# Looking up the chosen expert numbers with 16 operations of 50 candidates instead of three operations on a table of 800

## The reference, cut to what matters

```python
s1 = jnp.einsum('nhd,hkd->nhk', q[..., :PEER_HALF], k1)
s2 = jnp.einsum('nhd,hkd->nhk', q[..., PEER_HALF:], k2)
sc1, i1 = lax.top_k(s1, PEER_TOPK)
sc2, i2 = lax.top_k(s2, PEER_TOPK)
cand = (sc1[..., :, None] + sc2[..., None, :]).reshape(blk, PEER_HEADS, PEER_TOPK * PEER_TOPK)
top_sc, top_c = lax.top_k(cand, PEER_TOPK)
e1 = jnp.take_along_axis(i1, top_c // PEER_TOPK, axis=-1)
e2 = jnp.take_along_axis(i2, top_c % PEER_TOPK, axis=-1)
experts = e1 * N_KEYS + e2
gate = jax.nn.softmax(top_sc, axis=-1)
u_sel = u_tab[experts]
act = jax.nn.gelu(jnp.einsum('nd,nhkd->nhk', xt, u_sel).astype(jnp.float32), approximate=False)
z = (gate * act).astype(xt.dtype)
return jnp.einsum('nhk,nhkd->nd', z, v_tab[experts])
```

## Time and profile before

| | |
|---|---|
| median of three runs | 1917.72 us (1914.35 to 1924.69) |
| span of the profiled execution | 1749.2 us |
| the rest of the median, outside the span | 168.5 us |
| busy in the span: PE, DVE, ACT, POOL | 1093.8, 1073.7, 340.8, 1060.4 us |
| moved by the DMA engines | 659.75 MB, mean 377 GB/s |

### The profile page before, as it was taken

The page is one execution under the profiler, slowest core; times in us unless marked ns, Lnnn a source line. Parts: engine busy times, 40 slices in busy tenths (PEclk is TensorE's granted clock), DMA queues, the critical chain, the costliest instruction groups (busy, mean ns, idle before and its releaser), DMA issues.

```text
span 1749.2 us, 18263 instructions
## 1 busy us (share of the span) xinstructions
PE 1093.8 (63%) x6249; PEld 668.8 (38%) x6249; DVE 1073.7 (61%) x2724; ACT 340.8 (19%) x883; POOL 1060.4 (61%) x1131
## 2 busy tenths in 40 slices
PE   7968758988797989888853337743333333333344
PEld 6867736866675687566620001100000000000001
DVE  5636698765598187654347484848485757575420
ACT  3413223654132146403110000010000000000000
POOL 2005266665444566755567776677777777777771
PEclk9989878988898999989986568856666555665558
DMA  6579999899999999999999999999999999999997
GB/s 191 174 230 405 409 407 367 327 372 409 375 321 387 410 408 409 409 365 409 410 409 365 385 393 365 382 398 410 409 410 409 410 409 410 410 409 410 409 409 283
DMA packets 192850, 659.75 MB, mean 377 GB/s; under 512 B 32336, under 2 KB 32344, under 8 KB 192632
## 3 DMA queue, kind: packets, MB, share of 16 engines
q0 software_dynamic: 156672, 570.49, 83.2%
q1 hardware_dynamic: 35512, 86.01, 13.9%
q10 hardware_dynamic: 576, 2.10, 0.3%
HBM read 652.96 MB, written 5.16 MB: 376 GB/s over the span
## 4 chain that ended last, share of the span: by engine, by line
DMA 29%; PE 24%; POOL 21%; DVE 12%; issue 9%; ACT 2%; SPq 2%; ACTq 0%; POOLq 0%; DVEq 0%
POOL ring L609 15%; DMA ring<-in_u_experts,expert_idx 12%; PE pp L650 9%; DMA ring<-in_v_experts,expert_idx_by_token 7%; PE y L925 6%; DVE ring L1100 5%; PE pp L660 3%; PE pp L730 2%; POOL C_sample L609 2%; SPq L496 2%; DMA act_T<-in_v_experts,expert_idx_by_token 1%; POOL w_ring L609 1%; DMA w_ring<-in_w_all 1%; DMA w_ring<-in_u_experts,expert_idx 1%; DMA act_T<-in_u_experts,expert_idx 1%
## 5 line engine op out<-in xcount | busy, mean ns | idle before, releaser
L1100 DVE SCALAR_TENSOR_TENSOR ring<-ring,x_normed 128x1024 f32<-128x1024 f32 x440 | 530.1, 1219 | 345.2 <-DMA ring<-in_u_experts,expert_idx 341.0
L609 POOL DMA_INDIRECT ring<-in_u_experts,expert_idx x472 | 452.7, 959 | 399.0 <-DVE expert_idx L1480 123.7
L925 PE MATMUL y<-ring,z_columns 128*32 128x512 f32 x1328 | 411.5, 794 | 232.4 <-DMA ring<-in_v_experts,expert_idx_by_token 169.8
L609 POOL DMA_INDIRECT ring<-in_v_experts,expert_idx_by_token x308 | 304.7, 989 | 160.1 <-issue 75.0
L650 PE MATMUL pp<-act_T,w_ring 128*128 128x128 f32 (+2 forms) x1728 | 299.1, 332 | 43.5 <-DMA w_ring<-in_w_all 13.5
L650 PEld LDWEIGHTS pp<-act_T,w_ring 128*128 128x128 f32 x1728 | 266.3, 200 | 84.2 <-issue 49.6
L925 PE MATMUL y<-C_sample,z_columns 128*32 128x512 f32 x352 | 233.0, 926 | 66.0 <-DMA ring<-in_v_experts,expert_idx_by_token 51.8
L925 PE MATMUL y<-w_ring,z_columns 128*32 128x512 f32 x180 | 137.5, 984 | 181.6 <-DMA ring<-in_v_experts,expert_idx_by_token 161.5
L925 PEld LDWEIGHTS y<-ring,z_columns 128*32 128x32 f32 x1328 | 78.0, 131 | 400.0 <-issue 396.6
L660 PE MATMUL pp<-w_ring,act_T 128*128 128x128 f32 (+1 forms) x832 | 107.1, 291 | 27.8 <-DVE scratch L1297 10.8
L925 PEld LDWEIGHTS y<-w_ring,z_columns 128*32 128x32 f32 x180 | 21.4, 152 | 268.1 <-issue 268.1
(11 more groups left out here) (305 smaller groups left out, 1525.1 us busy)
## 6 DMA issues: line engine op xcount, KB each, us to landing
w_ring<-in_w_all SPq DMA_DIRECT2D x144, 512.0 KB, 6.9
ring<-in_u_experts,expert_idx POOLq DMA_INDIRECT x472, 11.0
ring<-in_v_experts,expert_idx_by_token POOLq DMA_INDIRECT x308, 10.0
x_res<-in_x_prompt SPq DMA_DIRECT2D x4, 512.0 KB, 7.9
C_sample<-in_state_C SPq DMA_DIRECT2D x4, 512.0 KB, 14.0
out_C_s<-C_sample ACTq DMA_DIRECT2D x4, 512.0 KB, 11.5
out_y_p<-x_res SPq DMA_DIRECT2D x16, 128.0 KB, 5.3
C_sample<-in_v_experts,expert_idx_by_token POOLq DMA_INDIRECT x80, 12.0
```

The source lines that it names most:

```text
L609: pool.indirect_dma_start(out=slot[s], out_offset=None, in_=a["u_experts"] if kind == "u" else a["v_experts"], in_offset=bass.IndirectOffs ...
L925: ins = pe.matmul(Y[low:low + 32, half * 512:(half + 1) * 512], zcols[:, part % 2, lo:lo + 32], rhs, start=False, stop=True, skip_group_ch ...
L1100: dve.scalar_tensor_tensor(out=slot[s], in0=slot[s], scalar=1.0, in1=xn_now[:, :] if t else xs[:, :], op0=ALU.mult, op1=ALU.mult, accum_ou ...
```

## The change

For each head, the two operations on a 16 x 50 table (compare, multiply) and the sum over it give way to one operation for each of the 16 picks. It compares the 50 positions with this pick's position, which comes as a scalar of one value per partition, multiplies by the 50 expert numbers, and adds up its own output through `accum_out` into the pick's place in `eid`. The waits between the three operations go, and one wait behind the sixteen stays.

```diff
             def experts_of(t, part, heads):
 
-                shape = [128, TOPK, CAND]
                 for h in heads:
-                    step(dve.tensor_tensor(hit, bc(iota[:, :], 1, shape), bc(posf[:, h, :], 2, shape), ALU.is_equal))
-                    step.done()
-                    step(dve.tensor_tensor(hit, hit, bc(ceid[:, h, :], 1, shape), ALU.mult))
-                    step.done()
-                    step(dve.tensor_reduce(eid[:, h, :], hit, AX.X, ALU.add))
+                    for k in range(TOPK):
+                        step(dve.scalar_tensor_tensor(out=hit[:, k, :], in0=iota[:, :], scalar=posf[:, h, k:k + 1], in1=ceid[:, h, :],
+                                                      op0=ALU.is_equal, op1=ALU.mult, accum_out=eid[:, h, k:k + 1]))
                     step.done()
                     between()
```

## The result

The changed kernel takes 1940.09 us (median of 6 runs, 1930.21 to 1946.03). The kernel before takes 1914.42 us (6 runs, 1902.76 to 1924.69, the three of the table ahead among them). The ratio is 1.0122, with a 95% interval of 1.0091 to 1.0152: about 23 us slower, and more than the 0.5% that a measurement can tell. The forecast was 1918.0 us and "same".

What follows compares the result with a forecast made beforehand. The gathers' start plus their bytes at a 409 GB/s DMA ceiling, plus losses below it, bounded the kernel. Adding 0.2 to 0.7 us for look-ups and subtracting up to 2.2 for POOL, little believed, gave 1918 us, range 1907 to 1935.

Steps and rivals of the forecast that it cites:

- The price of the new look-up alone: DVE's look-up: one operation every 0.188 us, 3.11 us a head against 3.07, 1.4 us more DVE work over 34 heads.
- a read that costs 0.07 us: Rival in DVE's look-up: the accumulator's read takes its own time, operations 0.255 us apart, 1923 to 1937 us; chance 0.15.
- no overlap: Rival in DVE's look-up: each operation waits for the previous read's end, 0.37 us each, 1932 to 1969 us; chance 0.08.
- the scalar is hidden: Rival in DVE's look-up: the scalar's load comes free, operations 0.127 us apart, 1902 to 1914 us; chance 0.06.
- the forecast of no change: Whole kernel: time the same within about 0.5% (9.6 us), at 1918 us; chance 0.74.
- the first line of "How the numbers follow": Whole kernel: 168.5 us lie between the profiled span of 1749.2 us and the median of 1917.7 us.
- 409 GB/s is what this traffic gets: DMA engines: 409 GB/s is the gathers' ceiling, held for the last third of the kernel.
- what DVE loses there is taken up: Between 1000 and 1200 us: POOL is ahead, so free slots absorb DVE delays of a few microseconds.
- The late look-ups: Twelve look-ups after 1040 us: on the recorded chain, but taken as running beside a full DMA queue.
- The sum: DVE's look-ups: 1.4 us more work over 34 heads, of which 0.2 to 0.7 us reach the end.
- bounded at 5 to 18 look-ups of 34: Look-ups before 560 us: five on the chain and 13 behind 265 us; between 5 and 18 pass their change on.

Runs made afterwards that it cites:

- e14: The changed kernel again, unedited, on a chip where the kernel before takes 1749.04 us: 1745.86 us, ratio 0.9992.
- e3: The changed kernel with its sixteen operations a head without accumulator, and one reduction over the table behind them: 1935.24 us, ratio 1.0102 to the kernel before.
- e0: The kernel before, unedited, profiled again on a chip of the slower kind: 1923.09 us, span 1921.3 us.
- e9: The kernel before with gathers of a quarter of each row's bytes (layer not computed): 1893.44 us, ratio 0.9885.
- e8: The kernel before with the sixteen operations only in the last nine parts (18 heads), the old look-up ahead of them: 1928.32 us, ratio 1.0060.
- e1: The kernel before with 29 added one-element multiplications behind each head's three look-up operations: 1951.83 us, ratio 1.0173.
- e4: The changed kernel with only the last of a head's sixteen operations incrementing the semaphore: 1942.66 us, ratio 1.0159 to the kernel before.
- e2: The kernel before with the first operation of each head's look-up done three times: 1933.87 us, ratio 1.0073.
- e5: The kernel before with the sixteen operations only in parts 0 to 7 (16 heads), the old look-up afterwards: 1924.37 us, ratio 1.0063.
- e7: The kernel before with its three look-up operations on two-byte integers and one more cast a part: 1919.54 us, ratio 1.0034.
- e11: The kernel before with a two-byte table and one look-up for both heads of a part: 1925.22 us, ratio 1.0042.
- e10: The changed kernel with gathers of a quarter of each row's bytes (layer not computed): 1915.89 us, ratio 0.9993 to the kernel before.
- e12: The kernel before with plain transfers of adjacent rows instead of indirect gathers (layer not computed), where before takes 1747.70 us: 1724.72 us, ratio 0.9877.
- e13: The changed kernel with plain transfers instead of indirect gathers (layer not computed), where before takes 1747.70 us: 1734.79 us, ratio 0.9916.
- e15: The changed kernel with plain transfers instead of indirect gathers, run again where before takes 1749.04 us: 1728.56 us, ratio 0.9894.

## Why the prediction was wrong

**The price of the new look-up alone was right.** One operation every 0.188 us was forecast, and 0.192 is what both traces of the changed kernel show where DVE isn't held up; 3.11 us a head against 3.19; DVE busy 1.4 us more against 7.8 (1081.5 us in e14, 1073.7 in the trace of before); the first gather 0.0 to 0.1 us later against 0.12. The accumulator's read costs 0.011 us start to start (0.192 against 0.181 in e3), where 0.004 were read from the earlier trace rows, and the operation with a scalar does need 0.13 us beyond its elements, as read from the earlier trace rows. The rivals "a read that costs 0.07 us", "no overlap" and "the scalar is hidden" were wrong in their mechanism, whatever time they gave: each of them says that the operations start evenly 0.25, 0.37 or 0.13 us apart. On a chip of the kind that the earlier trace rows came from, the forecast of no change held: 0.9992, with 409 GB/s behind 1200 us.

**The step that failed is the first line of "How the numbers follow".** It took 168.5 us as time outside the span and carried it over. In every run since, of either kernel and of the experiments, 1.7 to 2.6 us lie outside. A span of 1749.2 could not belong to runs of 1917.7, and the two stood side by side in the table. I read it as a constant. It was the difference between two conditions in which this kernel runs, and the timed one had never been profiled. Added back as a constant, it brought the time of the kernel before out right, and so hid that every term of the change had been read in the other condition. That the earlier trace rows were taken in the 1748-us condition is worked out from spans, rates and waits that agree with e14's; that run's own time isn't known.

**With it fell the bound.** "409 GB/s is what this traffic gets" and "what DVE loses there is taken up" hold in the 1748-us condition. In the timed one the rate behind 1200 us is 370 GB/s for the kernel before (e0) and 367 with the change, POOL is not ahead (from 1200 to 1700 us its waits of over 0.31 us come to 62 us in e0, and the trace of before has none), and quartering the bytes gives 1.2% (e9). The late look-ups, which I had taken for covered, carry about half of the loss (e8: 11.5 us, interval 6 to 17).

**And a price was missing from the sum.** The timelines of the earlier trace rows show small instructions in a run without a hole, and I costed sixteen of them and their reads by those rows. In the timed condition a run of small DVE instructions is held to one in 1.40 or 0.70 us at times, and the holes come to 69 us where the three long operations wait 8.6 us (e0). The sum had +1.4 us of DVE time and nothing for holes; measured are 11.8 us of busy time and 60 us of idle time more, 72 us. That small instructions are enough for holes, without scalar or accumulator, e1 shows; that the increments don't matter, e4; that holes go with a time beyond DVE's own work, e1 beside e2. Their number alone doesn't give the size: 0.033 us of holes an instruction in e1 and 0.036 in e3, but 0.064 with the accumulator's reads in between (one trace each), so a part of the accumulator in it isn't excluded.

**The size is explained in part.** By e2, where 66 us of plain work gave 14 us (8 to 20), the 72 us make 15 us (9 to 22), an estimate. Measured are 23 us (17 to 29). The rest has no run that shows it. It may be the same that e5, e7 and e11 have: they lie 6 to 12 us above before with 3 us of holes ahead of small instructions (e5) or no such instructions at all, and e7 and e11 with less DVE time than before. How much each place passes on was bounded at 5 to 18 look-ups of 34, or 0.15 to 0.53; e2 has 14/66 = 0.21.

**Many small tiles.** The Trainium skill ("VectorE: DVE Perf Modes", the errata section) speaks against many small tiles, for a fixed latency that each pays. The trace agrees: of the 0.192 us from one operation to the next, 0.052 are its 50 elements, and 0.14 us, sixteen times, are 2.2 us a head. The exchange comes out level even so, 3.19 us a head against 3.07, because the sixteen run over 800 elements in all and the three over 800 each. The loss on the timed chips is another one: 11 us of holes in the late head shown above and none in the first, where a fixed latency would be the same in both.

**What stays open.** What holds DVE up. The instructions wait for nothing in the profile. It struck most where POOL issued gathers back to back, but it struck in e10 with a quarter of the bytes, too, so the volume is not it. In the late head shown above no transfer that loads instructions ran: of the queues of kind "instruction", the last one started at 1439.2 us and the next at 1478.2. PE's weight loads have a trace of it: the 640 loads of 128x128 at L660 waited 60.5 us for "issue" in the trace of after and 55.3 in e0, but 22.2 in the trace of before and 19.7 in e14. PE's matmuls wait 184 us for "issue" in e0 and 6 us in the trace of before, so whatever it is, it isn't DVE's alone. The holes could be late delivery of the instructions or late completion; in the "remote" waits it is the semaphore's update that is recorded late. What would tell POOL's indirect gathers from the rest, plain transfers on a chip where before takes 1915 us, wasn't tried: e12, e13 and e15 all ran on the other kind. And what makes a chip one of the one kind or the other, or whether it stays so, isn't shown by any run. No version here beats both kernels: e7 (1.0034) and e11 (1.0042) come nearest where before takes 1915 us, and on the other chips the change itself is level.

## What to carry to other kernels

Before building a sum on a trace, set its span beside the timed runs. Where they differ by more than the few microseconds that lie outside a span, the trace is of another condition, and its bounds and waits are not those of the time to be forecast. Count instructions as well as their time: replacing three long Vector operations by 32 short ones of the same total cost nothing on one kind of chip and 1.2% on the other. The place to look is a dense run of short instructions. And before a difference between two traces is put down to a change, profile the unchanged kernel on the same chip: POOL's waits for dot products up to 900 us seemed to have grown by 41 us, and e0 had them, too.

## What the runs showed of the hardware

The same program has two levels of time by chip: the kernel before takes 1914.56 to 1920.78 us on three of them and 1747.70 to 1749.04 us on two, at nearly the same granted clock (0.767 in e0, 0.775 in e14). The difference of some 170 us comes with waits whose semaphore is updated late: on DVE 174 us in 39 waits (e0) against none, 102 us of them for its own finished work and 72 for PE's, and such waits on ScalarE and GpSimd, too. A longest wait of 9.5 us at one of those lines recurs in several traces, with a quarter of the bytes as well (e9).

In the slower of the two conditions consecutive small DVE instructions, where held up, mostly start 1.40 us apart, or 0.70 us (70 of the 93 held up in the look-ups of after); the two values are the same ahead of an operation of 50 elements, of a read of one, and of e1's multiplications of one element (9 and 21 of 44).

A multiplication of 800 two-byte elements took 577 ns (e7), against 991 with four bytes, but the comparison beside it, whose picks are repeated along the innermost dimension, took 989 ns, as with four bytes, and the reduction 986.
